# Two-layer hybrid attention step: exponentials taken from the first score product and turned by a product with a diagonal matrix, instead of a second score product

## The reference

```python
s = jnp.einsum('bqkgd,blkd->bkgql', qblk, k)          # scores of 128 queries with all their keys
if sink is not None: s = concatenate([s, sink column])
p = jax.nn.softmax(s, axis=-1)                         # over keys; the sink's share is dropped afterwards
out = jnp.einsum('bkgql,blkd->bqkgd', p, v)
```

## Time and profile before

| what | value |
|---|---|
| median of 3 runs | 1519.32 us (1518.76 to 1519.97) |
| the profiled execution: its own time | 1520.94 us |
| its span, first to last instruction | 1519.1 us |
| mean granted clock of PE | 0.986 of full speed |
| PE matmul busy | 1445.8 us (95%), 8776 instructions |
| PE weight loads busy | 1306.1 us (86%) |
| DVE busy | 796.1 us (52%) |
| POOL busy | 771.7 us (51%) |
| ACT busy | 587.9 us (39%) |

### The profile page before, as it was taken

How to read it: one execution, slowest core, us unless ns; L and a number is a source line. 1 busy time by engine, 2 the same in 40 slices (tenths; PEclk the granted TensorE clock), 3 DMA queues, 4 the chain that set the end, 5 groups by cost and what they waited for, 6 DMA issues and landing times.

```text
span 1519.1 us, 21747 instructions
## 1 busy us (share of the span) xinstructions
PE 1445.8 (95%) x8776; PEld 1306.1 (86%) x8776; DVE 796.1 (52%) x1164; ACT 587.9 (39%) x934; POOL 771.7 (51%) x554
## 2 busy tenths in 40 slices
PE   5999999999998999999979999998999999999996
PEld 3898889889887888999868988897988879999985
DVE  4675676452677520312784747764436775022157
ACT  4334564233764311213243346542357632222140
POOL 2454676323676443344674557753246755443443
PEclk9999999999999999999999999999999999999998
DMA  8412000212000443444320220012110013215221
GB/s 336 126 56 74 29 28 21 90 47 83 28 29 28 132 156 122 141 159 139 124 98 28 88 70 15 29 56 73 56 57 28 29 53 113 76 62 198 96 99 70
DMA packets 36756, 126.90 MB, mean 84 GB/s; under 512 B 5040, under 2 KB 5680, under 8 KB 36656
## 3 DMA queue, kind: packets, MB, share of 16 engines
q1 hardware_dynamic: 29952, 108.54, 21.3%
q10 hardware_dynamic: 6704, 16.97, 3.1%
HBM read 119.73 MB, written 5.77 MB: 83 GB/s over the span
## 4 chain that ended last, share of the span: by engine, by line
PE 87%; DVE 5%; POOL 3%; issue 2%; ACT 2%; DVEq 0%; POOLq 0%; ACTq 0%
PE ps L910 46%; PE ps L858 7%; PE ps L860 7%; PE ps L859 7%; PE ps L1045 3%; PE ps L1043 2%; PE ps L1095 2%; PE ps L1072 2%; PE ps L1071 2%; PE ps L1092 2%; PE ps L1093 2%; PE ps L927 1%; POOL w_lo L1764 1%; DVE o_inv L1633 1%; PE ps L1102 1%
## 5 line engine op out<-in xcount | busy, mean ns | idle before, releaser
L1764 POOL TENSOR_TENSOR w_lo<-raw,w_hi 128x1024 fp32r<-128x1024 f32 x148 | 360.1, 2440 | 359.0 <-ACT w_hi L1138 358.7
L910 PE MATMUL ps<-h_hi,w_hi 128*128 128x320 f32 x1280 | 299.3, 315 | 18.4 <-DVE g_c L1645 8.0
L910 PE MATMUL ps<-h_hi,w_lo 128*128 128x320 f32 x1280 | 292.6, 310 | 0.0
L910 PE MATMUL ps<-h_lo,w_hi 128*128 128x320 f32 x1280 | 292.6, 310 | 0.0
L1792 POOL TENSOR_TENSOR p_lo<-p_f,p_hi 128x512 fp32r<-128x512 f32 x164 | 211.9, 1296 | 139.0 <-ACT p_hi L1298 138.2
L910 PEld LDWEIGHTS ps<-h_hi,w_hi 128*128 128x128 f32 x1280 | 217.3, 189 | 39.3 <-DVE g_c L1645 9.8
L910 PEld LDWEIGHTS ps<-h_lo,w_hi 128*128 128x128 f32 x1280 | 215.9, 189 | 2.2
L910 PEld LDWEIGHTS ps<-h_hi,w_lo 128*128 128x128 f32 x1280 | 215.6, 189 | 2.2
L1138 ACT ACTIVATE w_hi<-raw 128x1024 fp32r<-128x1024 f32 x148 | 152.8, 1051 | 92.1 <-DMA raw<-in_weights 53.7
L1589 DVE TENSOR_REDUCE top<-ps 128x1 f32<-128x512 f32 (+1 forms) x128 | 83.7, 658 | 144.7 <-PE ps L1050 105.0
L1660 DVE TENSOR_TENSOR gy<-ps,sg 128x640 f32<-128x640 f32 x32 | 26.4, 824 | 241.2 <-PE ps L910 241.1
(11 more groups left out here) (180 smaller groups left out, 2599.2 us busy)
## 6 DMA issues: line engine op xcount, KB each, us to landing
raw<-in_weights SPq DMA_DIRECT2D x190, 512.0 KB, 3.4
raw_more<-in_weights SPq DMA_DIRECT2D x10, 512.0 KB, 10.6
x<-in_x_sample ACTq DMA_DIRECT2D x6, 512.0 KB, 8.0
x_mid<-x ACTq DMA_DIRECT2D x5, 512.0 KB, 2.6
x<-x_mid ACTq DMA_DIRECT2D x5, 512.0 KB, 6.5
y_sample<-x SPq DMA_DIRECT2D x3, 512.0 KB, 2.6
pack<-in_pack ACTq DMA_DIRECT2D x2, 528.0 KB, 4.8
x<-in_x_sample SPq DMA_DIRECT2D x2, 512.0 KB, 4.9
```

The lines of the kernel that those rows point to most:

```text
L910: last = pe.matmul(ps[:, s + half, 0:HALF], w[:, u % RING, cols], acts[:, k, half * HALF:(half + 1) * HALF], start=k == 0 and part == 0, s ...
L1764: did(pool.tensor_tensor(w_lo[:, n % RING, :], raw_tile(r), w_hi[:, n % RING, :], ALU.subtract), w_ready)
```

## The change

The second score product goes. After `S` of one unit, ACT takes the exponential from the same bank, with the negated maximum as the bias of each query and the sum over the keys as a second output (`ex`). The exponentials of a whole group lie in `p_f`, queries on the partitions. DVE takes the reciprocal of the four sums (`iv`), POOL multiplies the identity by it, for each head a diagonal matrix `dg`. A step then is `T`: for each head one product of the 128 x 128 tile of `p_f` with the head's diagonal, which turns the tile and divides by the sum in one. Both operands are plain fp32, not the rounded format. ACT rounds the result to `p_hi`, DVE (not POOL) takes `p_lo` from the bank (`pl`). `PV` has two products, with [v_hi | v_lo] side by side as one stationary tile: p_hi, then p_lo. The two halves of the result are added by ACT (a copy of the upper half) and DVE. The sink only adds to the sum, so its steps go, and so do the mask products of `ST`, the `row` events, the ones and the memsets that made them. One stage of filler moves from ahead of the attention into its first units (z 1 in a, gate 3 in b). Weight splits are held back between a group's last score unit and its `iv`. The lag from a step to its `PV` is two steps, not three.

```diff
-                    elif kind == "ST":
...
-                        pe.matmul(ps[:, s, :], k_hi[:, kv, key], q_t[:, heads, tokens], start=True, stop=False)
-                        last = pe.matmul(ps[:, s, :], k_lo[0:TOP_ROW + GRP, kv, key], q_m[0:TOP_ROW + GRP, n % 3, :],
-                                         start=False, stop=mask is None)
-                        if mask is not None:
...
-                            last = pe.matmul(ps[:, s, :], ident_r[:, :], mask_r[:, block:block + 1, :].to_broadcast([P, GRP, P]),
-                                             start=False, stop=True)
+                    elif kind == "T":
+                        _, l, br, g, i = e
                         s = begin(e)
+                        n = NO[("iv",) + e[1:4]]
+                        pe.wait_ge(dg_made, n + 1)
+                        for h in range(GRP):
+                            last = pe.matmul(ps[:, s, h * P:(h + 1) * P], p_part(br, g)[:, h, i * P:(i + 1) * P], dg(n)[:, h, :],
+                                             start=True, stop=True)
                         did(last, filled[s])
...
+                        values = vv[:, key, kv, :, :].rearrange("p s d -> p (s d)")
+                        pe.matmul(ps[:, b, :], values, p_hi[:, n % 3, :], start=i == 0, stop=False)
+                        wait_drained(pe, ("T",) + e[1:])
+                        last = pe.matmul(ps[:, b, :], values, p_low(br, n), start=False, stop=ends)
```

ACT, the exponential of a score unit (in branch a the cached keys are first copied out of their bank, and each head has a second exponential from the copy):

```diff
+                    elif kind == "ex":
+                        _, l, br, g, i = e
+                        scores, unit, c = ("S",) + e[1:], score_units(br, g)[i], NO[("iv",) + e[1:4]]
+                        s = wait_filled(act, scores)
...
+                        act.wait_ge(neg_made, NEG_NO[scores])
+                        if unit == "cache":
+                            did(act.activation(cached[:, g % 2, :], ps[:, s, :], ACT.Copy), drained[s])
+                            continue
+                        if br == "b" and unit in ("heads", GRP - 1):
+                            act.wait_ge(es_d_made, ES_NO[scores])
+                            act.activation(sums[:, c % 3, 1, :], es_d[:, c % 3, :], ACT.Exp)
+                        for h in range(GRP) if unit == "heads" else (unit,):
+                            p, bias = p_part(br, g)[:, h, :], neg[:, c % 3, h:h + 1]
...
+                            last = act.activation(p, src, ACT.Exp, bias=bias, accum_out=sums[:, c % 3, 0, h:h + 1])
+                        did(last, drained[s])
```

DVE and POOL:

```diff
+                            after(did(dve.tensor_reduce(best[:, h:h + 1], ps[:, s, 0:n * P], axis=AX.X, op=ALU.max)))
+                            other = others[:, h:h + 1] if br == "a" else sinks[:, h:h + 1]
+                            did(dve.tensor_scalar(neg[:, c, h:h + 1], best[:, h:h + 1], other, -1.0, ALU.max, ALU.mult), neg_made)
...
+                        if br == "b" or GROUPS[g][1]:
+                            after(did(dve.tensor_tensor(total, total, sums[:, c, 1, :], ALU.add)))
+                        did(dve.reciprocal(inv[:, c, :], total), inv_made)
+                    elif kind == "pl":
...
+                        did(dve.tensor_tensor(p_low(br, n), ps[:, s, :], p_hi[:, n % 3, :], ALU.subtract), drained[s])
...
-                        after(did(dve.reciprocal(o_inv[0:HD, cols], ps[sums, b, cols])))
...
+                            last = dve.tensor_tensor(og_sum(n)[head_rows(odd), :, :], by_head(ps[0:HD, b, :])[:, odd:GRP:2, :],
+                                                     by_head(o_low[HD:P, n % 2, :])[:, odd:GRP:2, :], ALU.add)
...
+                        did(pool.tensor_tensor(dg(n)[:, :, :], ident.unsqueeze(1).to_broadcast([P, GRP, P]),
+                                               inv[:, n % 3, :].unsqueeze(2).to_broadcast([P, GRP, P]), ALU.mult), dg_made)
```

The order of the events of attention (with `lag` 2 and `ahead` 3; `holder` is the group whose buffer this group takes over):

```diff
+        start = -1 if holder < 0 else first[holder + 1] - 1
+        end = max(first[g] - ahead, start)
         for i, e in enumerate(units):
...
+            at = start + (end - start + 1) * i // len(units)
...
+            scores[at].append(e)
+            exps[at].append(("ex", *e[1:]))
+        inverses[end if end < 0 else end + 1].append(("iv", l, br, g))
...
     for n, (g, i) in enumerate(steps):
-        out.append(("ST", l, br, g, i))
-        out.extend(early[n])
+        out.append(("T", l, br, g, i))
+        out.extend(scores[n])
+        out.append(("pl", l, br, g, i))
         tick()
         if n >= lag:
             product(n - lag)
         fill()
+        out.extend(inverses[n])
+        out.extend(exps[n])
```

More of the change, by code:

```diff
@@ L38 @@
 CACHE = T
-SINK = T + 1
 KEY_TILES = T + 2
@@ L42 @@
 FRONT = 0
-TOP_ROW = 96
 HF_ACT = 4
@@ L52, with group_slots, p_place @@
 FIRST_MODS = (0, 4, 1, 5, 2, 6, 3, 7)
-def key_slots(br, tile):
-    last = [(SINK, None)] if br == "b" else []
+def group_slots(br, g):
+    tile = GROUPS[g][1]
     if tile == 0:
-        return [(0, None)] + last
+        return [0]
     if br == "a":
[L62 to L68, removed]
+        return [1, 2, 3, 4, CACHE]
+    return {1: [CACHE, 1, 2], 2: [CACHE, 1, 2, 3], 3: [2, 3, 4, CACHE], 4: [3, 4, CACHE]}[tile]
+def p_place(g):
+    return (g % 2, 0, g - 2) if g < 2 * T - 2 else (0, g - (2 * T - 2), 2 * T - 4)
 def score_units(br, g):
@@ L92, in whole, with attention @@
     return chunks(stage, 1) + [stage]
-def attention(l, br, filler, last_filler, lag, row_ahead, score_ahead):
+def attention(l, br, first_filler, filler, last_filler, lag, ahead):
     count = len(GROUPS)
@@ L102, in attention @@
     first = [steps.index((g, 0)) for g in range(count)]
-    early = {n: [] for n in range(-1, len(steps))}
-    start = -1
+    scores = {n: [] for n in range(-1, len(steps))}
+    exps = {n: [] for n in range(-1, len(steps))}
+    inverses = {n: [] for n in range(-1, len(steps))}
     for g in range(count):
         units = [("S", l, br, g, u) for u in range(len(score_units(br, g)))]
-        end = max(first[g] - score_ahead, -1)
+        holder = p_place(g)[2]
+        start = -1 if holder < 0 else first[holder + 1] - 1
+        end = max(first[g] - ahead, start)
         for i, e in enumerate(units):
[L109 to L115, removed]
+            at = start + (end - start + 1) * i // len(units)
+            assert at >= -1 and (holder < 0 or at >= first[holder + 1] - 1)
+            scores[at].append(e)
+            exps[at].append(("ex", *e[1:]))
+        inverses[end if end < 0 else end + 1].append(("iv", l, br, g))
     filler = list(filler)
-    places = len(steps) + len(early[-1])
+    places = len(steps)
     out, later, used = [], [], [0, 0]
@@ L289, in layer_order @@
                 ("qt", l, "b", 0)])
-    for c in range(KT_B):
+    for c in range(KT_B - 1):
         out.extend(whole(gate("b", c)))
@@ L293, in layer_order @@
     filler = []
[L294 to L298, removed]
+    for br, c in [("b", KT_B - 1), *((br, c) for br in "cu" for c in range(KT_B))]:
+        filler.extend(chunks(gate(br, c), 6))
+        filler[-1] = (filler[-1], gate(br, c))
+    out.extend(flat(attention(l, "b", filler[:6], filler[6:-3], filler[-3:], 2, 3)))
     out.append(("pool", 0, 1, 2, 3, 4, 5, 6, 7))
@@ L393, in with_splits @@
 def with_splits(order, freed, lag):
-    count, out, due, turn, started = len(freed), [], {}, RING, False
+    count, out, due, turn, started, held = len(freed), [], {}, RING, False, False
     for e in order:
@@ L403, in with_splits @@
         started = started or e == ("split", RING - 1)
[L404 removed]
+        if e[0] == "S" and e[4] == len(score_units(*e[2:4])) - 1:
+            held = True
+        if e[0] == "iv":
+            held = False
+        if e[0] in ("mm", "cr", "h", "T", "mix", "oc", "kc", "qc"):
             for n in due:
                 due[n] -= 1
[L407 removed]
+            while started and not held and turn in due and due[turn] <= 0 and not (freed[turn - RING][:2] == ("oc", 0)):
                 out.append(("split", turn))
@@ L1639, in _ @@
+                            did(last, drained[b] if odd else None)
                     elif kind == "gT" and e[2] == "u":
```

292 lines of the change are left out of this document (122 added, 170 removed).

## The result

The changed kernel takes 1613.05 us (median of 4 runs, 1603.71 to 1614.44), the kernel before on the same chip 1519.04 (4 runs, 1516.89 to 1519.97). The ratio is 1.0608, with a 95% interval of 1.0566 to 1.0650: slower by 94 us. The forecast was 1523 us with a range of 1510 to 1541, so it is wrong, by far, and on the side that it held for likelier. None of its rivals comes near either. One execution of w_nohold (1811 us at a clock of 0.75) fell into a slow state of the chip and is left out.

A forecast was written before the change was run, and what follows sets the result against it. The prediction took PE to bound the kernel: PE work +8.2, waits that go -22.8, waits that come +18.2, in sum +3.6 us on the profiled execution, so 1523 us as median, range 1510 to 1541.

The forecast's parts named there:

- PE work that comes: On PE in attention: T's plain fp32 products, two instructions each, 144 x 8 x 0.1115 = 128.4 us.
- rivals A and B: A, the forecast: work up, waits exchanged, 1516 to 1532, chance 0.45; B: branch starts hidden, 1511 us, chance 0.27.
- PE work, net +8.2: On PE in attention: 128.4 us of T come, 120.2 us of score, PV, mask and sink products go.
- two instructions: In T: each plain fp32 product takes two PE instructions of 0.1115 us, so 0.892 us a step.
- rival E: In T: one instruction to a product instead of two, 1523 - 64 = 1459 us, chance 0.03.
- Waits that go, -22.8: PE's waits for read-outs, maxima and key tiles, with the half clock behind them, disappear: 22.8 us less.
- `g_c` by DVE, `g_c` by ACT and `top_r`: PE's waits for filler read-outs, 8.0 us by DVE and 6.0 by ACT, and for maxima, 1.1, go.
- The fills: DVE's constant fills ahead of the key tiles go, removing PE's later key-tile wait and half clock: 3.6 us.
- Waits that come, +18.2: PE's new waits at filler stages, branch starts and in the stream, for exponentials and diagonals: 18.2 us.
- Term (1): Filler stages c in b: PE waits about 0.8 us for ACT's table load and SiLU, eight times: 6.4 us.
- rival D: At SiLU stages and starts of b: each ACT table switch costs PE a second 1.28 us, 1538 us, chance 0.05.
- Rival C: The diagonal is late in every group, 0.6 us for each of 32 groups: 1542 us, chance 0.20.

The follow-up runs named there:

- w_nohold: a_wide without holding the weight splits back between a group's last score unit and its diagonal: 1527.85 us, ratio 1.0046 to the kernel before.
- b_s64: The kernel before with one line changed, the second product of each score unit on 64 rows instead of 96: 1585.14 us, ratio 1.0432.
- a_ahead: The changed kernel, 64-row pairs kept, with the moved filler stage (z 1, gate 3) whole ahead of the attention again: 1628.33 us.
- a_group: The changed kernel with the four k_hi products of each four-head score unit first, then the four 64-row k_lo products: 1572.61 us.
- a_f32r: The changed kernel, 64-row pairs kept, with both operands of T in the rounded format: 1561.07 us (1551.14 to 1569.68).
- a_wide: The changed kernel with the second score product on all 128 rows, and the upper half of O copied in two pieces: 1515.56 us, ratio 0.9971.
- w_ahead: a_wide with the moved filler stage (z 1, gate 3) whole ahead of the attention again: 1541.78 us.

## Why the prediction was wrong

**The step that failed** is the first of its sums, "PE work that comes". It lists T and nothing else, and looks for a bound from above only for T. The score product that stays has no term, as if unchanged, though its line in the diff goes from TOP_ROW to HD: it went from 96 rows to 64, and 224 pairs of S change between 128 and 64 rows twice each. b_s64 puts that at +65.6 us in the kernel before, 77 for the pairs less the waits and the half clock that went with them. In the changed kernel taking it out is worth 97.5: 74 for the pairs and 31 for the half clock, less 8 of waits. The 31 is an estimate from the two traces, whose kernels differ in the rows and in the copy that makes room for them; that the half clock goes with the 64 rows is what the runs show. Why the pairs pull the clock down beside T (0.967) and not beside ST (0.992) stays open: a_ahead shows that the wait for the last key tile isn't needed for it, a_group that fewer changes bring part of it back (0.984), and a_f32r didn't decide.

**The rest of the sum**, read on a_wide, the changed kernel without that step: forecast 1523, measured 1515.6, between the forecasts of rivals A and B. The total is near because terms that were too high on both sides cancel.

- *PE work, net +8.2.* Added up over all records, the distances from start to start are 117.2 us for T, and 7.1 more for the S product that follows it (a T's last distance is short, the next product's long); 116.7 us less stand on the lines of ST, PV and masks. The forecast had 128.4 that come and 120.2 that go; both are some 4 us high, and the net of +7.6 is right. So is "two instructions" (1152 on the line of T, rival E out).
- *Waits that go, -22.8.* `g_c` by DVE, `g_c` by ACT and `top_r` went, with the half clocks behind them (1.00 over 366 to 480). The fills were mis-read: the wait at the start of a stays without them and grows from 1.9 to 3.3 us over both layers ("issue"; w_ahead, which puts filler in front of it, takes it away), and the half clock behind it grows too (0.57 over 126 to 134, before over 124 to 128, so 1.7 more). The 3.6 us for the fills didn't go and some 3 came, so about 16 of the 22.8 were gained.
- *Waits that come, +18.2.* 7.0 us came: 4.5 for exponentials, 2.5 for diagonals. Term (1), 6.4 us for eight SiLU stages, is nothing. The working put the table load behind the last piece of filler; ACT does it ahead, while it is idle, and only 0.70 us is left under T and PV. The rows are of the changed kernel; a_wide has the same (load 385.06, SiLU 388.54):

```profile
421.31 1.28 ACT L1336 ACT_TABLE_LOAD   x1
425.57 0.70 ACT L1336 ACTIVATE g_c<-ps 128x640 f32<-128x640 f32 x1 [2.98 <-PE ps L931]
426.29 1.28 ACT L1301 ACT_TABLE_LOAD   x1
427.59 0.69 ACT L1301 ACTIVATE p_f_b<-ps,neg 128x512 f32<-128x512 f32 x1
428.17 0.19 ACT L1301 ACTIVATION_READ_ACCUMULATOR p_f_b<-ps,neg 128x1 f32 x1
```

  The rows that it rested on the earlier trace rows show the load right behind another operation, on an ACT that was late then. Here the load starts without waiting for the product that the SiLU waits for (2.98 us more); whether it is on the path depends on how far ahead of PE ACT is.
- *The table loads.* ACT does load the other table right behind the SiLU (426.29), as rival D has it, but PE doesn't wait for it: its list has no wait for `g_c` and 2.1 us in all for exponentials of b. D is out. The drain that the Trainium skill has for a switch ("ScalarE: Activation LUTs", section What ACT_TABLE_LOAD costs) doesn't show here either: the second load starts straight behind the SiLU's end at 426.27, the exponential at 427.59 straight behind the load. The measurement decides.
- *Rival C.* Its condition (over 0.9 us for an exponential with its sum) is nearly met, 0.69 and 0.19 for reading the sum, yet PE waits for a diagonal four times, not in 32 groups. w_nohold has 12 us more when POOL isn't kept free. The diagonal itself took 1.04 us where 1.30 was taken.

As read on a_wide the sum is 7.6 - 16 + 7.0 = -1.4 us; measured are some -4 (1515.56 against 1519.32 or 1519.63), so 2 to 3 us are not attributed.

## What to carry to other kernels

Read the shapes on both sides of a diff, above all on lines that "only lose a name", and cost the instructions that stay as well as those that come and go; a stationary tile of 64 rows between tiles of 128 cost 0.33 us here, one of 65 or 96 rows nothing. When PE is busy for more time with fewer waits, compare the distance from start to start of the same product in both traces before looking for a wait. And ask of every plain fp32 product whether it must multiply: a division done on an engine with room turned two instructions into one and gave 52 us.

## What was not expected of the hardware

- A change between a stationary tile of 64 rows and one of 128 costs 0.14 to 0.15 us beyond the product itself within a pair (512 columns 0.84 us for 0.54, 128 columns 0.51 for 0.22), whatever the columns, and up to 0.17 with what falls on the product behind (74 to 77 us for 448 changes); at 65 rows nothing.
- PE at 1.2 GHz for some 25 us while its busy time fills the whole stretch (0.52 over 925 to 950). The busy share alone doesn't tell whether the clock is up.
- An exponential with a sum as second output brings an instruction of 0.19 us of its own (ACTIVATION_READ_ACCUMULATOR), the same for 128 and for 512 columns.
- The division of a 128 x 512 tile on POOL with a broadcast operand took 1.04 us, the subtraction into the rounded format on the same engine 1.30.
